# Convolving feed-forward stage: splitting weight units one unit sooner, and forming the low parts of the down units by accumulating transfers

## The reference

```python
def causal_dwconv(x, w, bias):          # 3 taps along the tokens, channel by channel
    y = lax.conv_general_dilated(x, w[:, None, :], ..., padding=((CONV_WIDTH - 1, 0),), ...)
    return y + bias

h2 = rmsnorm(x, norm_ffn_g[i])                                  # 256 x 1024
up = causal_dwconv(h2 @ w_up[i], conv_w[i], conv_b[i])          # 256 x 5632
g_ff, v_ff = up[..., :D_FF], up[..., D_FF:]                     # 2816 each
x = x + (jax.nn.silu(g_ff) * v_ff) @ w_down[i]                  # 2816 -> 1024
```

## Time and profile before

| | |
|---|---|
| runs, median of three | 1596.63 us |
| profiled execution | 1597.49 us |
| its span on the core | 1595.7 us |
| TensorE matmuls busy | 1569.8 us (98%) |
| DVE busy | 1093.0 us (68%) |
| ACT busy | 867.9 us (54%) |
| transfers, mean | 195 GB/s |
| accumulating transfers | 25, of 1 MB |
| the convolving stage | from about 282 us to about 473 us of the span |

### The profile page before, as it was taken

The page is one execution under the profiler, slowest core; times in us unless marked ns, Lnnn a source line. Parts: engine busy times, 40 slices in busy tenths (PEclk is TensorE's granted clock), DMA queues, the critical chain, the costliest instruction groups (busy, mean ns, idle before and its releaser), DMA issues.

```text
span 1595.7 us, 22459 instructions
## 1 busy us (share of the span) xinstructions
PE 1569.8 (98%) x9010; PEld 1367.4 (86%) x9010; DVE 1093.0 (68%) x1418; ACT 867.9 (54%) x999; POOL 74.4 (5%) x65
## 2 busy tenths in 40 slices
PE   8998999999999999999999999999999999999998
PEld 6987998888888888898888888888888988888886
DVE  7779948788778666654757666676666547576665
ACT  8877584665575444554446444554445544464443
POOL 1112100000000000011100000000000101000000
PEclk9999999999999999999999999999999999999999
DMA  7999995455556555454445555455554535455551
GB/s 292 279 252 255 283 254 208 159 217 182 191 182 237 187 183 189 160 190 148 184 142 206 211 183 188 158 211 191 181 195 164 187 139 187 148 207 211 185 191 74
DMA packets 44255, 310.60 MB, mean 195 GB/s; under 512 B 4992, under 2 KB 5376, under 8 KB 7296
## 3 DMA queue, kind: packets, MB, share of 16 engines
q1 hardware_dynamic: 39696, 279.87, 48.2%
q0 software_dynamic: 3600, 26.22, 8.1%
q10 hardware_dynamic: 864, 3.15, 0.6%
HBM read 308.17 MB, written 1.05 MB: 194 GB/s over the span
## 4 chain that ended last, share of the span: by engine, by line
PE 88%; DVE 7%; ACT 2%; DMA 1%; issue 1%; SPq 0%; POOL 0%; POOLq 0%; DVEq 0%; ACTq 0%
PE pairs L855 22%; PE pairs L862 11%; PE pairs L640 9%; PE pairs L641 9%; PE pairs L642 9%; PE big L640 7%; PE big L642 7%; PE big L641 7%; PE pairs L876 2%; DVE wlo L570 2%; DVE ar L1830 2%; PE pairs L884 1%; DVE ar L1838 1%; DMA wlo<-weights 1%; PE big L691 1%
## 5 line engine op out<-in xcount | busy, mean ns | idle before, releaser
L570 DVE TENSOR_TENSOR wlo<-raw,whi 128x2048 fp32r<-128x2048 f32 x235 | 538.7, 2304 | 177.3 <-ACT whi L556 175.1
L556 ACT ACTIVATE whi<-raw 128x2048 fp32r<-128x2048 f32 x260 | 494.0, 1910 | 126.4 <-PE big L642 62.8
L855 PE MATMUL pairs<-h_both,whi 128*128 128x512 f32 x1600 | 408.0, 393 | 0.4 <-DVE wlo L570 0.3
L855 PEld LDWEIGHTS pairs<-h_both,whi 128*128 128x128 f32 x1600 | 290.6, 189 | 52.8 <-DVE wlo L570 1.3
L862 PEld LDWEIGHTS pairs<-h_both,wlo 128*128 128x128 f32 x1600 | 218.3, 191 | 15.6
L1379 ACT ACTIVATE ar<-pairs 128x512 f32<-128x512 f32 x133 | 78.9, 595 | 272.4 <-PE pairs L855 223.5
L862 PE MATMUL pairs<-h_both,wlo 128*128 128x256 f32 x1600 | 223.3, 283 | 0.0
L640 PE MATMUL big<-whi,b_hi 128*128 128x512 f32 x452 | 177.8, 393 | 0.5 <-DVE wlo L570 0.4
L642 PE MATMUL big<-whi,b_lo 128*128 128x512 f32 x452 | 176.5, 390 | 0.0
L641 PE MATMUL big<-wlo,b_hi 128*128 128x512 f32 x452 | 176.2, 390 | 0.0
L1830 DVE TENSOR_TENSOR ar<-pairs,ar 128x512 f32<-128x512 f32 (+1 forms) x124 | 90.9, 733 | 102.9 <-ACT ar L1379 88.6
(11 more groups left out here) (248 smaller groups left out, 2020.6 us busy)
## 6 DMA issues: line engine op xcount, KB each, us to landing
raw<-weights SPq DMA_DIRECT2D x262, 1024.0 KB, 4.8
wlo<-weights POOLq DMA_DIRECT2D x25, 1024.0 KB, 14.9
ar<-consts ACTq DMA_DIRECT2D x1, 2112.0 KB, 12.2
ar<-mem SPq DMA_DIRECT2D x2, 512.0 KB, 5.5
raw<-weights SPq DMA_DIRECT2D x4, 256.0 KB, 6.2
x_rows<-x SPq DMA_DIRECT2D x1, 1024.0 KB, 10.9
out<-ar SPq DMA_DIRECT2D x2, 512.0 KB, 2.7
ar<-ssm_bc SPq DMA_DIRECT2D x1, 512.0 KB, 14.0
```

What stands on the lines that cost most here:

```text
L556: act.activation(whi[:, slot(u), :], raw[:, u % RING, :], ACT.Copy).then_inc(S("hi_done"), 1)
L570: dve.tensor_tensor(wlo[:, slot(u), :], raw[:, u % RING, :], whi[:, slot(u), :].bitcast(F32), ALU.subtract)\
L855: return pe.matmul(out, w(k, l, (half * KD + kk) * P, P)[0], h_both[:, kk, :, :].rearrange("p a t -> p (a t)"), start=kk == 0, stop=kk == ...
```

## The change

ACT and DVE split one unit further ahead in the convolving stage: the argument of each split in the loops grows by one, the first pair of up units gets a third split, one split moves to the head of ACT's and ahead of the first taps on DVE, and the last split of the stage falls away on both. And the list `LO_BY_DMA` gains ten units: D1 to D7 (`U_MIX1 + 3i + 4` for i = 1 to 7) and D8 to D10 (`U_BLOCK1 - 3` to `U_BLOCK1 - 1`); `U_BLOCK1` was in it before.

```diff
-LO_BY_DMA = [*range(7, 31), U_BLOCK1]
+LO_BY_DMA = [*range(7, 31), *(U_MIX1 + 3 * _i + 4 for _i in range(1, NI - 3)), *range(U_BLOCK1 - 3, U_BLOCK1 + 1)]
+LO_MIX1 = 24
...
-            for u in LO_BY_DMA[:-1]:
+            for u in LO_BY_DMA[:LO_MIX1]:
                 add_raw(u)
...
             norm(2)
-            add_raw(U_BLOCK1)
+            for u in LO_BY_DMA[LO_MIX1:]:
+                add_raw(u)
...
                     if conv:
                         up_copy(par, done)
                         conv_first(par, f, used)
-                        split_act(act, k, l)
+                        split_act(act, k + 1, l)
                         conv_silu(par, f + 1)
...
                     if conv:
+                        split_act(act, k0, l)
                         up_copy(0, used[0])
                         conv_first(0, 0, ua)
                         up_copy(1, used[1])
-                        split_act(act, k0, l)
+                        split_act(act, k0 + 1, l)
                         conv_first(1, 1, ub)
                         conv_silu(0, 1)
                         conv_silu(1, 2)
+                        split_act(act, k0 + 2, l)
+                        return
...
                     if i < NI - 2:
-                        split_act(act, k + 2, l)
+                        split_act(act, k + 2 + conv, l)
+                if conv:
+                    return
                 split_act(act, k0 + U_FFN - 3, l)
-                if last or conv:
+                if last:
                     return
...
                         taps(par, f)
                         if f == 2 * NI - 1:
                             gate(i, par)
-                        split_dve(dve, k, l)
+                        split_dve(dve, k + 1, l)
...
                     up_sum(0, 1)
+                    split_dve(dve, k0, l)
                     if conv:
                         taps(0, 0)
-                        up_sum(1, 2)
-                        split_dve(dve, k0, l)
+                    up_sum(1, 2)
+                    if conv:
                         taps(1, 1)
-                    else:
-                        split_dve(dve, k0, l)
-                        up_sum(1, 2)
                     gate(0, 0)
                     gate(0, 1)
                     split_dve(dve, k0 + 1, l)
+                    if conv:
+                        split_dve(dve, k0 + 2, l)
...
                     if i < NI - 2:
-                        split_dve(dve, k + 2, l)
+                        split_dve(dve, k + 2 + conv, l)
+                if conv:
+                    return
                 split_dve(dve, k0 + U_FFN - 3, l)
-                if last or conv:
+                if last:
                     return
```

## The result

| | before | after |
|---|---|---|
| median of four runs | 1596.56 us | 1628.48 us |
| lowest and highest | 1596.15, 1597.27 | 1627.86, 1630.02 |
| ratio, with its 95% interval | | 1.0199 [1.0187, 1.0212] |
| span of the profiled execution | 1595.7 us | 1626.7 us |
| mean granted clock of TensorE | 0.996 | 0.988 |

The change costs 31.9 us. The forecast was 1629 us, in a range of 1607 to 1645, with 0.86 on slower.

The account below looks back on a forecast made before the run. TensorE, busy 98% of the span, was taken as the bound. Terms 9.8 + 8.4 + 7.8 - 1.8 + 8.5 = +32.7 us on 1597.49 gave 1630.2 profiled, 1629 us as median; range 1607 to 1645.

Parts of the forecast that it names:

- D1, 9.8 us: Start-up of the stage: TensorE wants D1 at 326.0, its low part lands at 335.8, so it waits 9.8 us.
- The landing: Accumulating transfers in the stage: from POOL's issue to the low part's arrival, taken as 12.5 us, ends 9.2 and 14.9.
- D3, D5 and D7, 2.8 us each: Steady part: low part there at T + 19.4, wanted at T + 16.61; three waits of 2.8, 8.4 us together.
- T + 6.94: Steady part: POOL issues the transfer 6.94 us after T, the end of the up unit that frees the down unit's slot.
- the even ones: D2, D4, D6: no wait, since the wait before gives the next transfer 19.4 us; D2 because ACT and DVE catch up.
- D8, D9 and D10, 7.8 us: Stage's tail: D8 waits 2.4 us; D9 and D10 2.7 each, DMA engines needing 8.1 us per unit against TensorE's 5.43.
- the second copy: ACT: ten added negated copies of 1.92 us each; the steady part has room for what queues behind them.
- The pauses that go, 1.8 us: TensorE's old pauses of 0.16, 0.68, 0.44 and 0.51 us vanish with earlier splits; the 0.71 before D0 stays.
- The clock, 8.5 us: TensorE's granted clock falls to the lower level after waits, costing 8.5 us in all; bounds 0 and 10.2.
- The five charges of 1.7: Lower clock: 1.7 us each for D1, D3, D5 and D7, and once for D8 to D10, from two 2 us windows.
- The sign that I had named: TensorE in the stage: if right, the clock is under 1.00 in a window behind each wait.
- rival 2: Stage's transfers land in the shortest time, 9.2 us; steady part clean, D1 waits 6.5; 1609 us, chance 0.14.

## Why the prediction was right

*D1, 9.8 us.* 9.20. Its parts hold nearly to the tenth: POOL was to issue at 323.3 and TensorE to want D1 at 326.0, on the clock of the trace before. This stage began 0.83 us earlier, so 322.5 and 325.2; the rows are 322.44 and 334.41 - 9.20 = 325.21. The landing took 11.9 instead of 12.5. The two pauses between D0 and D1 did go; what they gave back only made this wait longer, which the sum had on both sides.

*D3, D5 and D7, 2.8 us each.* 2.50, 3.51 and 2.63: 8.6 for 8.4 (behind the 3.51 is a landing of 12.9 us, behind the others 11.9). The issue at T + 6.94 was at T + 6.82, and that the even ones would wait for nothing came out, and was shown by leaving the odd ones out. The landing, the one number that the trace before left open, was 11.9 in the middle instead of 12.5; TensorE wanted the unit 0.36 us sooner after T than one triple, and these two small errors are of opposite sign.

*D8, D9 and D10, 7.8 us.* 7.6, but **here the step failed and the sum came out by luck**. I had 2.4, 2.7 and 2.7; measured were 1.08, 2.07 and 4.47. For D8 the issue came at T + 6.4 and the landing took 11.0, both less than I had. For D9 and D10 I put the bound in the DMA engines alone. It is there in part (landings grow from 11.0 to 12.0 and 14.1 as two transfers overlap), but the issues also stand 6.4 us apart, a turn of ACT with two copies in it. I had costed the second copy at nothing, which holds in the triples and not in the tail.

*The pauses that go, 1.8 us.* All four went in the change. As a gain of the early split alone this does not hold: it removes the 0.51 before D10, but DVE's third split of the start-up pushes the gates of unit 3 back, and the 1.99 us of pauses there become 2.43. D0's pause grew from 0.71 to 0.85.

*The clock, 8.5 us.* 8.1 by the balance of the stage, 8.2 by TensorE's busy time (in the kernels without new transfers or copies this lies between 1566.4 and 1569.8 us, so it is a rough check), 7.7 in the launch with the gaps filled. The five charges of 1.7 are right in sum and not one by one: 1.4 to 1.7 behind D1, D3, D5 and D7, nothing behind D8 and D9, 2.4 behind D10. The sign that I had named, a clock under 1.00 behind each wait, is missing at D8 and D9. Both windows that I had added up for the 1.7 stand behind the first of the two gaps; behind the second the clock was 0.61 and 0.53 in two windows of 2 us, 1.7 us again.

*The rivals.* The landing that decides was between rival 2 (9.2) and the forecast (12.5), near the latter. By the fit of the Trainium skill ("DMA: Bandwidth & Descriptors", section "Anatomy of one DMA — SWDGE (gpsimd) path") it would have been 4.4 us, an estimate by that page, and the change free. None of the eleven in this stage landed under 10.4 us, so for an adding transfer the measurement decides, against the page. What in the transfer takes the rest was not tried.

## What to carry to other kernels

When work moves from an engine to a transfer, count from the moment the buffer comes free, over the steps that issue it, to the landing, and hold that against the same stretch of the consumer; how idle the DMA engines are says little. Take the landing from a transfer of the same kind in the trace, since a plain load took 4.8 us where an adding one took 11.9. A unit that waits for nothing may owe it to the wait before it, and a wait on TensorE can cost more than its length: here 1.4 to 1.7 us of clock behind waits of 2.50 to 3.51 us, 2.7 to 3.0 behind waits of 4.83 to 4.98, nothing behind one of 2.07, and only 1.6 behind the one of 9.20. How long the wait is does not tell it alone.

## What I had not expected

A gap on TensorE can be filled with matmuls whose result nobody reads, and the launch gets 7.7 us shorter (1628.48 to 1620.79), though the first transfer it waits for comes no sooner. Second, pauses at the start-up that change their releaser and their place with the order of TensorE's products and keep their sum (1.99 and 1.97 us, and 2.43 and 2.42 with the split sooner); only work put into DVE's own idle places made them go.
